# Norm by token tiles, products in order of arrival, and a new order of the step from the dense to the expert stage

## The reference

```python
x_n = rms_norm(x, mix_norm_g); h = x_n @ w_in
y_a = (a_gb * conv3(a_gc * a_val)) @ w_out_a
y_b = silu(layer_norm(conv31(glu(h_glu)))) @ w_out_b + b_out_b
y_x = cross_attention(q, rms_norm(mem), w_kv) @ w_out_x
x = x + (g0 * y_a + g1 * y_b + g2 * y_x) @ w_o
z = rms_norm(x, ffn_norm_g)
# top-1 group of 4 (softmax), top-2 of its 8 experts, weights combine[token, expert]
for e in range(32):
    gate, up = split(z @ w_gate_up[e])
    y = y + combine[:, e] * ((silu(gate) * up) @ w_down[e])
out = rms_norm(x + y, final_norm_g)
```

## Time and profile before

| what | us |
|---|---|
| median of 3 runs | 878.83 (877.76 to 878.89) |
| the profiled execution | 878.62 |
| its span, first to last instruction | 876.8 |
| busy: PE, DVE, ACT, POOL | 850.4, 788.4, 646.6, 21.9 |
| mean granted clock of TensorE | 0.993 of full |

### The profile page before, as it was taken

One profiled execution on the slowest core, in us unless ns is written; L12 is line 12 of the kernel. 1 busy time (PEld: TensorE's weight loads), 2 busy tenths in 40 slices (PEclk: granted clock), 3 DMA queues, 4 the chain that ended last, 5 costly groups with the idle time before them and its releaser, 6 DMA issues.

```text
span 876.8 us, 14484 instructions
## 1 busy us (share of the span) xinstructions
PE 850.4 (97%) x5711; PEld 754.2 (86%) x5711; DVE 788.4 (90%) x776; ACT 646.6 (74%) x611; POOL 21.9 (2%) x30
## 2 busy tenths in 40 slices
PE   5999999999999999989999999999999999999996
PEld 5999999999889999868788888888888888888874
DVE  5448999999977786869999999999999999999996
ACT  6574434344554466476999999999999999999995
POOL 0110000000000000033000000000000000000000
PEclk9999999999999999989999999999999999999998
DMA  9943545444452449635999999999999999999961
GB/s 377 416 166 127 191 178 205 164 162 183 166 192 96 160 176 392 265 136 203 376 423 427 425 430 430 429 428 427 427 431 430 428 428 425 430 431 430 427 265 49
DMA packets 20151, 270.70 MB, mean 309 GB/s; under 512 B 2192, under 2 KB 2448, under 8 KB 3856
## 3 DMA queue, kind: packets, MB, share of 16 engines
q1 hardware_dynamic: 19552, 268.06, 74.8%
q10 hardware_dynamic: 560, 2.10, 0.6%
HBM read 269.10 MB, written 1.05 MB: 308 GB/s over the span
## 4 chain that ended last, share of the span: by engine, by line
PE 82%; DVE 13%; issue 2%; ACT 1%; DMA 1%; SPq 0%; DVEq 0%; ACTq 0%
PE ps L1470 24%; PE ps L1484 12%; PE ps L1289 9%; PE ps L1290 9%; PE ps L1291 9%; PE ps L1457 4%; PE ps L1494 3%; DVE lo L1054 3%; DVE lo L805 3%; DVE conv L892 2%; PE ps L1306 2%; PE ps L1305 2%; PE ps L1304 2%; PE ps L1569 2%; PE ps L1576 1%
## 5 line engine op out<-in xcount | busy, mean ns | idle before, releaser
L1054 DVE TENSOR_TENSOR lo<-raw,hi 128x2048 fp32r<-128x2048 f32 x142 | 319.1, 2282 | 1.2 <-ACT hi L642 1.2
L642 ACT ACTIVATE hi<-raw 128x2048 fp32r<-128x2048 f32 x141 | 264.8, 1915 | 20.0 <-PE ps L1470 20.0
L1289 PE MATMUL ps<-inA,hi 128*128 128x256 f32 x576 | 164.3, 285 | 1.8 <-DVE lo L805 1.4
L805 DVE TENSOR_TENSOR lo<-raw,hi 128x2048 fp32r<-128x2048 f32 x62 | 142.5, 2301 | 24.0 <-ACT hi L436 22.6
L1290 PE MATMUL ps<-inA,hi 128*128 128x256 f32 x576 | 163.0, 283 | 0.0
L1291 PE MATMUL ps<-inA,lo 128*128 128x256 f32 x576 | 163.0, 283 | 0.0
L436 ACT ACTIVATE hi<-raw 128x2048 fp32r<-128x2048 f32 x63 | 120.5, 1913 | 56.3 <-PE ps L1291 37.6
L1470 PE MATMUL ps<-hi,xeT 128*128 128x512 f32 x384 | 154.4, 402 | 1.3 <-issue 0.9
L1470 PE MATMUL ps<-lo,xeT 128*128 128x512 f32 x384 | 150.2, 391 | 0.0
L1289 PEld LDWEIGHTS ps<-inA,hi 128*128 128x128 f32 x576 | 110.6, 192 | 3.3 <-DVE lo L805 3.2
L1290 PEld LDWEIGHTS ps<-inA,hi 128*128 128x128 f32 x576 | 110.7, 192 | 0.1
(11 more groups left out here) (246 smaller groups left out, 1254.6 us busy)
## 6 DMA issues: line engine op xcount, KB each, us to landing
raw<-in_w_experts SPq DMA_DIRECT2D x96, 2048.0 KB, 11.5
raw<-in_w_dense SPq DMA_DIRECT2D x29, 2048.0 KB, 7.8
raw<-in_w_dense SPq DMA_DIRECT2D x2, 1024.0 KB, 8.1
x_sb<-in_x SPq DMA_DIRECT2D x1, 1024.0 KB, 4.9
mem_sb<-in_mem SPq DMA_DIRECT2D x1, 1024.0 KB, 15.4
x_again<-in_x ACTq DMA_DIRECT2D x1, 1024.0 KB, 17.6
ffn_row<-in_rows ACTq DMA_DIRECT2D x1, 512.0 KB, 7.4
raw<-in_rows SPq DMA_DIRECT2D x1, 512.0 KB, 3.3
```

The source lines that it names most:

```text
L642: nc.scalar.activation(expert_half(hi, N0), raw_flat(slot, k % 2), ACT.Copy).then_inc(hi_made, 1)
L805: nc.vector.tensor_tensor(conv_half(lo, N), raw_half(slot, h), conv_half(hi, N).bitcast(f32), ALU.subtract).then_inc(lo_made, 1)
L1054: nc.vector.tensor_tensor(expert_half(lo, N0), raw_flat(expert_slot(m), k % 2), expert_half(hi, N0).bitcast(f32), ALU.subtract).then_inc(l ...
L1289: mm(dst, w_hi[:, k, c * P:(c + 1) * P], acts[:, 0, k, :], start=(k == 0), stop=False)
```

## The change

It has two parts, made together.

At the head, x is fetched in two DMAs, one for each tile, and each tile is squared, rooted, scaled and transposed by itself. The first high part of weights is a copy on VectorE, behind the scaling. The first two halves are multiplied in another order (`first_columns`): for half 0 high by high block by block as ScalarE delivers them, then low by high, then high by low as VectorE delivers; half 1 has the same products with the low activations ahead of the low weights.

In the transition, the last dense subtraction is taken ahead of the residual sum; the logits are split at two blocks instead of four; ScalarE's order is changed and its tables for root and silu are loaded elsewhere; `z_third` moves from POOL to VectorE; six seeds are run instead of four (banks 2 and 3 twice, with the same content); the first gather is made in three pieces (two, two and four blocks, in banks 4, 6 and 7) whose cutting starts piece by piece; the second `pick` comes later; the number of rounds is computed behind two subtractions of the expert stage; the tables of later rounds move to POOL. The waits count accordingly.

```diff
+        FIRST_GATHER = ((0, 2, 4), (2, 4, 6), (4, 8, 7))
+
+        def first_gathered_view(piece):
+
+            c0, c1, bank = FIRST_GATHER[piece]
+            return ps[:, bank, 0:(c1 - c0) * 2 * SLOTS].rearrange("p (c x s) -> p c x s", x=2, s=SLOTS)
...
-            sp.dma_start(x_sb[:, :, :], x.rearrange("(t p) d -> p t d", p=P)).then_inc(x_loaded, 16)
+            for t in range(TT):
+                sp.dma_start(x_sb[:, t, :], x[t * P:(t + 1) * P, :]).then_inc(x_tile_loaded[t], 16)
...
-            def z_third(g, t):
-
-                half_row = slice(g * 512, (g + 1) * 512)
-                pool.wait_ge(z_rest, 2 * g + t + 1)
-                pool.wait_ge(z_part1, 2 * g + t + 1)
-                nc.gpsimd.tensor_tensor(z_parts[:, 2, t, half_row], z_sb[:, t, half_row], z_parts[:, 1, t, half_row],
-                                        ALU.subtract).then_inc(z_part2, 1)
...
+            for r in range(1, MAX_ROUNDS + 1):
+                ins = nc.gpsimd.tensor_scalar(rank_tab[:, :, r * PAIRS:(r + 1) * PAIRS, :], rank_tab[:, :, 0:PAIRS, :],
+                                              -float(SLOTS * r), None, ALU.add)
+            ins.then_inc(rounds_made, 1)
...
-            act.wait_ge(x_loaded, 16)
             for t in range(TT):
+                act.wait_ge(x_tile_loaded[t], 16)
                 nc.scalar.activation(conv[:, 4 * t:4 * t + 4, :].rearrange("p a b -> p (a b)"), x_sb[:, t, :],
                                      ACT.Square, accum_out=stat[:, t:t + 1]).then_inc(sumsq, 1)
-            act.wait_ge(meansq, 1)
-            nc.scalar.activation(stat[:, 6:8], stat[:, 4:6], ACT.Sqrt).then_inc(root, 1)
-            dense_hi(0)
+                act.wait_ge(meansq, t + 1)
+                nc.scalar.activation(stat[:, 6 + t:7 + t], stat[:, 4 + t:5 + t], ACT.Sqrt).then_inc(root, 1)
             act.wait_ge(col_loaded, 16)
             for c in range(KT):
                 act.wait_ge(xT_turned, c // 2 + 1)
                 nc.scalar.activation(inA[:, 0, c, :], ps[:, 4 + c // 2, (c % 2) * T:(c % 2 + 1) * T], ACT.Copy,
                                      scale=vec("mix_g", c)).then_inc(x_hi, 1)
+            act.wait_ge(hi_made, 1)
...
+            def warm_root():
+
+                act.wait_ge(warm_used, 1)
+                nc.scalar.activation(stat[:, 23:24], stat[:, 23:24], ACT.Sqrt).then_inc(warm_used, 1)
...
-                     F["gate1"] + 3: [rank_constants], F["w_o"]: [load_ffn_row],
+                     F["gate1"] + 3: [rank_constants], F["w_o"]: [load_ffn_row, warm_root],
                      F["w_o"] + 1: [lambda: z_first(0, 0), lambda: z_first(0, 1), lambda: x2_square(0, 0), lambda: x2_square(0, 1)],
-                     F["w_o"] + 2: [lambda: x2_turned(0), lambda: x2_turned(1), lambda: z_second(0, 0), lambda: z_second(0, 1)]}
+                     F["w_o"] + 2: [lambda: z_second(0, 0), lambda: z_second(0, 1), lambda: x2_turned(0), lambda: x2_turned(1)]}
...
             x2_square(1, 0)
-            act.wait_ge(warm_used, 1)
-            nc.scalar.activation(stat[:, 23:24], stat[:, 23:24], ACT.Sqrt).then_inc(warm_used, 1)
+            z_first(1, 0)
             x2_square(1, 1)
-            z_first(1, 0)
-            z_first(1, 1)
-            act.wait_ge(meansq, 3)
-            nc.scalar.activation(stat[:, 6:8], stat[:, 4:6], ACT.Sqrt).then_inc(root, 1)
             x2_turned(2)
             x2_turned(3)
+            act.wait_ge(meansq, 4)
+            nc.scalar.activation(stat[:, 6:8], stat[:, 4:6], ACT.Sqrt).then_inc(root, 1)
+            z_first(1, 1)
             z_second(1, 0)
             z_second(1, 1)
             act.wait_ge(route_for_exp, 1)
             nc.scalar.activation(R["g_exp"], R["g_exp"], ACT.Exp).then_inc(route_exp, 1)
             dense_hi(DENSE + 2)
+            nc.scalar.activation(ident_bf[:, :], ident, ACT.Copy).then_inc(ident_made, 1)
+            nc.scalar.activation(minus_ident[:, :], ident, ACT.Copy, scale=-1.0).then_inc(ident_made, 1)
             act.wait_ge(route_for_exp, 2)
             nc.scalar.activation(R["diff"], R["diff"], ACT.Exp).then_inc(route_exp, 1)
+            act.wait_ge(warm_used, 2)
+            nc.scalar.activation(stat[:, 23:24], stat[:, 23:24], ACT.Silu).then_inc(warm_used, 1)
+            for piece, (c0, c1, _) in enumerate(FIRST_GATHER):
+                act.wait_ge(first_gathered, piece + 1)
+                nc.scalar.activation(xeT[:, 0, c0:c1, :, 0:SLOTS], first_gathered_view(piece), ACT.Copy).then_inc(first_xeT_hi, 1)
             act.wait_ge(x2_made, 4)
             expert_hi(0, 0, 3)
-            nc.scalar.activation(ident_bf[:, :], ident, ACT.Copy).then_inc(ident_made, 1)
-            nc.scalar.activation(minus_ident[:, :], ident, ACT.Copy, scale=-1.0).then_inc(ident_made, 1)
-            act.wait_ge(first_gathered, 1)
-            nc.scalar.activation(xeT[:, 0, 0:4, :, 0:SLOTS], gathered_bank(0), ACT.Copy).then_inc(first_xeT_hi, 1)
...
-            dve.wait_ge(sumsq, 2)
-            rstd(0, 4, 6, 20)
             for t in range(TT):
+                dve.wait_ge(sumsq, t + 1)
+                roots[0] += 1
+                nc.vector.tensor_scalar(stat[:, 4 + t:5 + t], stat[:, t:t + 1], 1.0 / D, EPS,
+                                        ALU.mult, ALU.add).then_inc(meansq, 1)
+                dve.wait_ge(root, roots[0])
+                link(nc.vector.reciprocal(stat[:, 20 + t:21 + t], stat[:, 6 + t:7 + t]))
                 nc.vector.tensor_scalar(x_sb[:, t, :], x_sb[:, t, :], stat[:, 20 + t:21 + t], None,
                                         ALU.mult).then_inc(scaled, 1)
+            dve.wait_ge(first_loaded, 16)
+            nc.vector.tensor_copy(conv_half(hi, 0), raw_half(raw_slot(0)[0], 0)).then_inc(hi_made, 1)
             dense_lo(0)
...
+
+            def z_third(g, t):
+
+                dve.wait_ge(z_rest, 2 * g + t + 1)
+                dve.wait_ge(z_part1, 2 * g + t + 1)
+                half_row = slice(g * 512, (g + 1) * 512)
+                nc.vector.tensor_tensor(z_parts[:, 2, t, half_row], z_sb[:, t, half_row], z_parts[:, 1, t, half_row],
+                                        ALU.subtract).then_inc(z_part2, 1)
...
                         if t == 0:
+                            if g == 1:
+                                dense_lo(n + 2)
                             dve.wait_ge(w_o_done, g + 1)
                         else:
-                            dense_lo(n + 2)
+                            if g == 0:
+                                dense_lo(n + 2)
+                            else:
+                                z_scaled(1, 0)
+                                z_third(0, 0)
                             dve.wait_ge(half_used, n + 1)
                         nc.vector.tensor_tensor(x2[:, t, 512 * g:512 * g + 512], ps[:, (n - 1 + t) % RING, :],
                                                 x_again[:, t, 512 * g:512 * g + 512], ALU.add).then_inc(x2_made, 1)
...
-            z_scaled(1, 0)
             z_scaled(1, 1)
+            z_remainder(1, 0)
             dve.wait_ge(sumsq, 8)
             link(nc.vector.tensor_reduce(stat[:, 8:10], stat[:, 0:4].rearrange("p (t g) -> p t g", g=2), AX.X, ALU.add))
             roots[0] += 1
             nc.vector.tensor_scalar(stat[:, 4:6], stat[:, 8:10], 1.0 / D, EPS, ALU.mult, ALU.add).then_inc(meansq, 1)
-            z_remainder(1, 0)
-            z_remainder(1, 1)
+            z_third(0, 1)
             dve.wait_ge(root, roots[0])
             link(nc.vector.reciprocal(stat[:, 20:22], stat[:, 6:8]))
+            z_remainder(1, 1)
...
             make_pick(0, slice(0, 1))
-            make_pick(1, slice(1, 2))
             dve.wait_ge(route_exp, 2)
             link(nc.vector.tensor_scalar(w1, diff, 1.0, None, ALU.add))
             nc.vector.reciprocal(w1, w1).then_inc(inverses, 1)
+            z_third(1, 0)
+            z_third(1, 1)
+            make_pick(1, slice(1, 2))
+
+            def first_xeT_lo(piece):
+
+                c0, c1, _ = FIRST_GATHER[piece]
+                dve.wait_ge(first_xeT_hi, piece + 1)
+                nc.vector.tensor_tensor(xeT[:, 0, c0:c1, :, SLOTS:2 * SLOTS], first_gathered_view(piece),
+                                        xeT[:, 0, c0:c1, :, 0:SLOTS].bitcast(f32), ALU.subtract).then_inc(first_xeT_made, 1)
+
+            for piece in range(3):
+                first_xeT_lo(piece)
+            expert_lo(0, 0, 2)
+            expert_lo(0, 0, 3)
             link(nc.vector.tensor_reduce(stat[:, 12:13], ps[:, 5, 2 * PAIRS:3 * PAIRS], AX.X, ALU.max))
...
-            expert_lo(0, 0, 2)
-            expert_lo(0, 0, 3)
-            for r in range(1, MAX_ROUNDS + 1):
-                ins = nc.vector.tensor_scalar(rank_tab[:, :, r * PAIRS:(r + 1) * PAIRS, :], rank_tab[:, :, 0:PAIRS, :],
-                                              -float(SLOTS * r), None, ALU.add)
-            link(ins)
...
+            dve.wait_ge(rounds_made, 1)
             dve.wait_ge(loops_made, 1)
...
-            pe.wait_ge(scaled, 2)
```

(80 more changed lines are left out.)

55 lines of the change are left out of this document (19 added, 36 removed).

## The result

The changed kernel takes 874.49 us (median of 5 runs, 873.12 to 874.69) against 877.86 for the kernel before (5 runs, 877.72 to 878.89): ratio 0.995, 95% interval 0.9939 to 0.9961, or 3.4 us less. The profiled executions differ by more, 873.8 against 878.62, spans 872.0 against 876.8: 4.8 us. The forecast was 872.0 in a range of 870.8 to 875.6. The sign and the range hold. The likeliest case promised 6.75 us, and the medians give half of it: 874.49 lies outside that case's own range of 871.2 to 873.0.

A forecast was written before the change was run, and what follows sets the result against it. TensorE bounds the dense stage, a gapless VectorE stream the expert stage from about 399 us. Head 3.15 plus transition 3.6 made 6.75 off 878.62, 871.9, median 872.0; range 870.8 to 875.6.

The forecast's parts named there:

- likeliest case: Whole kernel: head and transition gains both pass through, 6.75 us off, 872.0 us, own range 871.2 to 873.0; chance 57%.
- poor head: Rival, head: first products at low clock (1.1 us less), x tiles landing together (1.3) or slow copy (0.85); about 873.1; 14%.
- Head, 3.15 forecast: Program start to half 1: work by tiles and products in order of arrival start half 1 at 17.1, not 20.29.
- I put nothing on it; the bounds are 0 and 0.43: Head: one more DMA issue ahead of the first weights was costed at nothing, with 0.43 us the upper bound.
- a product takes 0.12 at full clock: Head: price of each first product; 34 behind the last high part of x put half 1 at 17.1.
- Transition, 3.6 forecast: Dense stage's end to expert stream: 3.25 us earlier, less 0.56 in the stream, plus 0.93 from the silu hole.
- the loop counts and round tables: Expert stream on VectorE: loop counts (1.29) enter it, round tables (0.73) leave for POOL; net cost 0.56 us.
- The silu hole: VectorE's hole of 0.93 us at 420.96, behind the silu table load on ScalarE's path, was to be gained.
- Third parts on VectorE: Transition: four third parts, about 0.65 us each, moved from POOL, hidden by a hair; without cover they cost 1.3.
- The clock falls under the logits: Rival, transition: TensorE's clock falls again, so rank products gain 0.4 us instead of 3.25; 874.9 us; 20%.
- 0.2 between profile and median: Total: the median of the runs was taken 0.2 us above the profiled execution, making 871.9 into 872.0.
- The dense stage swallows the head: Rival, dense stage: VectorE, busy 99.02 of 100 us there, absorbs the head's gain; 875.2 us; 4%.

The follow-up runs named there:

- e3: Changed kernel plus 22 products on a zeroed tile from program start and 8 before the first real products, keeping TensorE at work in the head: 873.49 us.
- e4: Changed kernel without the early load of the silu table; ScalarE loads it at the first silu, as before: 874.63 us.
- e1: Kernel before with only the head's edits, the transition left old: 876.66 us against 878.63.
- e5: Kernel of e3 with three more seeds, one ahead of the rank products and two between them and the gather: 872.54 us.
- e8: Kernel of e3 with four seeds instead of six: 874.14 us.
- e10: Kernel of e3 with the four third parts of z back on POOL: 874.58 us.
- e12: Changed kernel with 16 and 6 added head products, three more in transition waits, loop counts mostly on POOL, TensorE and ScalarE waiting for them only before the loop: 871.34 us.
- e11: Kernel of e3 with x fetched in one transfer, as in the kernel before, but still worked by tiles: 872.62 us.
- e7: Kernel of e3 with first transfers reordered: x tile 0, identity, x tile 1, first weights, columns, the other constants last: 873.12 us.

## Why the prediction was right, and where it was not

The sign is right and the time lies in the range; the sum is right in one half only. In the profiled execution 6.75 were forecast against 4.8: the transition gave a little more than its share, the head less than a third of its own. That the time still lies in the range is owed to the range's width. What came is not the case that had 57%; the rival "poor head", with 14%, had the cause, at two thirds of its cost.

- **Head, 3.15 forecast, 0.9 there.** The chain was right, its sizes were not. Squares, root, scaling, transposes and high parts started within 0.3 us of it; the copy took 1.23 for the forecast's 1.3 (the Trainium skill, "VectorE: DVE Perf Modes", "The perf-mode tier table", has 1227 ns, and the trace agrees). The 2.26 us that are missing at the logits are three terms. The low clock is 1.66 (after against e3, with the same copy time). The landing of the weights is 0.50 (e3 against e4), in the forecast the term "I put nothing on it; the bounds are 0 and 0.43"; in the changed kernel the copy started 0.73 behind the 9.47 of before, past the upper bound. 0.1 is left.
- **The step that failed** is the price of a first product, "a product takes 0.12 at full clock": the forecast saw the transposes at the low level and priced the products 1 us behind them at the high one. The rival "poor head" had the mechanism, but 1.1 us for it, because it had the 16 high ones end at 14.3; they took 3.78 and not 3.4 from a start 0.6 later, and the next 16 began at the low level too (2.56 instead of e3's 2.18). The rule beside it (the Trainium skill, "TensorE: Matmul & The Clock Gate", "What's actually happening": throttled by default, until activity releases it) is borne out by e3, where work from 1.22 us on brought the transposes down from 3.65 to 1.91. Which level an execution gets was not settled by it here: in e4 the first products were at the high level with no help, behind transposes at the low one, after 0.48 us of idle time, and in e1 they were at the low level after 0.53.
- **Landing of the weights.** With one transfer of x the first weights were in use at 9.38 and 9.47; with two the copy waited for them until 9.70 to 10.82 (e1, e4, after, e3, e5, e8, e10, e12). The queue that looked full was not full at its start (DMA share 0.60 before and 0.67 after, from 0 to 5 us), and with one issue more the weights were 0.2 to 1.4 later. That the issue itself is the cause is not shown: e11, with one transfer, says only that they were there by 9.85.
- **Transition, 3.6 forecast, 3.9 there.** Logits read 3.68 earlier against their start (forecast 3.3), rank products and gather the same (3.25), third subtraction 3.11: the loop counts and round tables cost 0.57 (0.56). The silu hole gave 0.8 (0.93); e4 shows that it was the table load, since the hole comes back with it. Clock 1.00 from 379 to 400, as forecast.
- **Third parts on VectorE, costed at nothing.** They were hidden, as forecast, and e10's trace shows more: on POOL they cost 1.1. The forecast had seen a cost on POOL only in the 3.09 of one subtraction.
- **Rivals.** "The clock falls under the logits" did not come in any trace with the new transition. It falls later, under the gather, in e4, e7 and e8, at 1.4 to 2.5 us each (transition column of the table, against 21.88). The forecast put 0.2 between profile and median; it was 0.7, and why is open. The other four executions of the changed kernel have mean clocks of 0.995 and 0.996 against 0.999, and a fall under the gather, as in e4 and e8, would lengthen them. But three are 0.7 to 0.9 longer than the profiled one, where it cost 1.4 in e4, and the fourth, with 0.995, took 873.12, less than the profiled one. An execution like e4's, with a better head and a slower gather, would fit better; there is no trace of any of the four. "The dense stage swallows the head" is ruled out: from the start of half 1 to the logits pass 358.8 us in before, after, e3 and e4 alike.

## What to carry to other kernels

- Price the first products after idle time at the low clock until a row shows the high one, and fill known waits of TensorE with products into a bank that is free. Here 22 + 8 of them gave 1.7 us in the head by the trace; with 16 + 6, and three more in the transition, all five executions of e12 had a mean clock of 0.997 or 0.998, where e3's had 0.995 to 0.999.
- A filling is cut to one wait. When the wait moves, the filling stands in the way: in e7 and e11 it held the first products back by about 1.3 us.
- Before moving an operation to another engine, list every wait on its semaphore. A result that was always early needs no thought as long as it stays early.
- An operation that nobody waits for on POOL can still lie on the critical path, by what it does to VectorE.

## What was not expected of the hardware

- The column of the granted clock reads 1.00 in the head while transposes take 0.228 and products 0.225 each, twice what they take later. It can't be used to tell the level at the start of a program; durations can.
- The level in the head changed at different times. The added products of 512 columns (0.43 low, 0.21 high from one to the next) turned to the high level at about 4.5 us in e3, 4.9 in e7 and 7.2 in e5, worked out from how long the 22 took; without them the first real products were low in after and e1 and high in e4, with equal rows until 9.3 us.
- POOL beside VectorE can stretch a small operation fivefold: 0.22 to 1.19 us for 4 elements in e10 (1.14 in e1), once in each, while its neighbour at 381.64 kept its 0.16. Subtractions of 2048 elements went from 2.28 to 2.35, and the one of the earlier trace rows to 3.09. The 0.97 more are less than one of POOL's two operations there (2.30 / 2 = 1.15), as if VectorE had waited for one of them to end; no run shows that it did.
- The first weights land up to 1.1 us apart (9.70 to 10.82) in kernels whose first transfers are the same, and the start of the logits moves with them: 0.62 and 0.64 later in e5 than in e3, 0.39 and 0.36 in e12.
